# Quarter-array products in the inverse of a delta-rule layer, and another order of work in its steps

## The reference, cut to what matters

```
def step(s, inp):
    r_t, w_t, k_t, v_t, kk_t, a_t = inp
    sa = jnp.einsum('bhvk,bhk->bhv', s, -kk_t)
    s = s * w_t[:, :, None, :] + sa[..., None] * (kk_t * a_t)[:, :, None, :] + v_t[..., None] * k_t[:, :, None, :]
    return s, jnp.einsum('bhvk,bhk->bhv', s, r_t)

o_f, s_f, k_f = direction(0, False, s_f0)
o_b, s_b, k_b = direction(1, True, s_b0)
o = o_f + o_b
```

## Time and profile before

| | us |
|---|---|
| median of 3 runs (1657.66 to 1657.81) | 1657.73 |
| the profiled execution | 1657.09 |
| its span, first to last instruction | 1655.3 |
| TensorE busy / VectorE / ScalarE / GpSimd in the span | 1465.5 / 605.6 / 528.1 / 264.7 |
| mean granted TensorE clock | 0.948 |
| the block of this change | 881 to 1235 |
| one pair of heads in the middle of it | 42.9 |

### The profile page before, as it was taken

How to read it: one execution, slowest core, us unless ns; L and a number is a source line. 1 busy time by engine, 2 the same in 40 slices (tenths; PEclk the granted TensorE clock), 3 DMA queues, 4 the chain that set the end, 5 groups by cost and what they waited for, 6 DMA issues and landing times. The chain is left out here.

```text
span 1655.3 us, 41184 instructions
## 1 busy us (share of the span) xinstructions
PE 1465.5 (89%) x17678; PEld 930.4 (56%) x17678; DVE 605.6 (37%) x1520; ACT 528.1 (32%) x1202; POOL 264.7 (16%) x260
## 2 busy tenths in 40 slices
PE   3998878878999999959998888888879779999997
PEld 1554557446555555535556777777755555555554
DVE  2003673243111111551214666666751511111116
ACT  3013553232121121220134666666541311111122
POOL 0000031002000000010034455556500100000010
PEclk9999899888999999979999999999988889999999
DMA  9324556737799999803210000000004469999992
GB/s 390 128 102 164 221 210 244 300 115 315 278 369 379 374 377 373 332 26 102 103 50 3 6 6 6 6 6 6 6 4 170 154 267 364 374 370 380 375 387 90
DMA packets 54037, 328.34 MB, mean 198 GB/s; under 512 B 6646, under 2 KB 10038, under 8 KB 18712
## 3 DMA queue, kind: packets, MB, share of 16 engines
q1 hardware_dynamic: 43632, 290.07, 45.9%
q0 software_dynamic: 5184, 18.88, 2.9%
q10 hardware_dynamic: 5096, 17.58, 2.7%
HBM read 304.35 MB, written 22.16 MB: 197 GB/s over the span
## 5 line engine op out<-in xcount | busy, mean ns | idle before, releaser
L1398 PE MATMUL ps<-ring,arena 128*64 128x256 f32 x2048 | 244.3, 387 | 6.0 <-ACT arena L1513 4.9
L1398 PEld LDWEIGHTS ps<-ring,arena 128*64 128x64 f32 x2048 | 142.4, 138 | 97.2 <-issue 36.6
L298 PE MATMUL ps<-HT,ring 128*128 128x384 f32 x544 | 181.3, 497 | 14.2 <-PEq L367 8.2
L298 PEld LDWEIGHTS ps<-HT,ring 128*128 128x128 f32 x544 | 105.8, 195 | 89.5 <-issue 20.3
L1408 PE MATMUL ps<-ring,arena 128*32 128x128 f32 x4096 | 133.9, 278 | 0.0
L1602 DVE TENSOR_TENSOR arena<-arena,ps 64x256 f32<-64x256 f32 (+1 forms) x128 | 40.6, 357 | 254.0 <-ACT arena L1519 254.0
L1434 PE MATMUL ps<-ring,arena 128*64 128x512 f32 x512 | 129.9, 605 | 0.0
L1518 ACT ACTIVATE arena<-ps 64x256 f32<-64x256 f32 x64 | 24.1, 377 | 311.3 <-PE ps L1398 311.3
L1408 PEld LDWEIGHTS ps<-ring,arena 128*32 128x32 f32 x4096 | 107.8, 111 | 27.0 <-issue 25.4
L298 PE MATMUL ps<-arena,ring 128*128 128x384 f32 x256 | 85.4, 498 | 18.8 <-DVEq L2053 18.8
L1526 ACT ACTIVATE arena<-ps 32x256 f32<-32x256 f32 x128 | 47.8, 374 | 160.3 <-PE ps L1434 159.2
(11 more groups left out here) (358 smaller groups left out, 2244.2 us busy)
## 6 DMA issues: line engine op xcount, KB each, us to landing
ring<-wstream SPq DMA_DIRECT2D x272, 1024.0 KB, 7.5
moe_rows<-arena ACTq DMA_DIRECT2D x28, 384.0 KB, 7.1
arena<-moe_tokens POOLq DMA_DIRECT2D x12, 512.0 KB, 14.7
moe_rows<-arena ACTq DMA_DIRECT2D x4, 512.0 KB
consts<-cst ACTq DMA_DIRECT2D x1, 1655.0 KB, 17.1
XT<-xT ACTq DMA_DIRECT2D x1, 1536.0 KB, 11.1
yT<-HT SPq DMA_DIRECT2D x3, 384.0 KB, 3.2
arena<-wa SPq DMA_DIRECT2D x1, 1024.0 KB, 4.9
```

Of the source, the lines that this page charges most:

```text
L298: mm = pe.matmul(bank(m % 8), w[:, k, m % 2 * P:m % 2 * P + P], rhs[:, k, :], start=k == 0, stop=k == KC - 1)
L1398: mm = pe.matmul(bank(h, 256)[HD * x:HD * x + HD], TOKE[:, k, 0:MANY], w[:, kk, x, :], start=k == 0, stop=k == KC - 1)
```

## The change

Five edits, all in this block.

1. `each` on halves of the array (12 matmuls, 64 rows, 64 columns out) becomes `quarters_pe`: 24 matmuls, each 32 rows by 32 columns, on the four tiles of the array's diagonal in turn; quarter q takes block q % 2 of head q // 2.
2. The masks of levels 1 to 4 are compacted once at the block's start from two 32-column halves to one (`LM`, 8 additions on VectorE), and `left_dve` and `right_dve` read and write 32 columns a chunk where they had 64.
3. ScalarE's decays of step 0 stand ahead of the copies L2226 and L2230 and not behind them.
4. In the steps of VectorE, the block masks of the next pair (L2318), the first sums (L2330, L2331), the addition of the unit matrix (L2335) and the transposition (L2336) stand in other places.
5. `first_level_dve` is cut in two, so that the transposition (`first_turn_dve`) has its own place.

```diff
+        PF = area(take(T), T, d=2, n=NCH, j=32)
+        LM = area(take(8 * 32), 8 * 32, v=4, d=2, j=32)
...
 def inverse_act
                     last.then_inc(s_vr, 1)
+                act.wait_ge(s_si[c % 2], c // 2 * 32 + 32)
+                act.wait_ge(s_zc, c + 1)
+                decays_act(act, c, 0)
                 act.wait_ge(s_inv, c * NINV + NINV - 2)
...
 def left_dve
-                mask = msk1(C_LEV + 2 * (n - 1) * CH, d)
-                dve.tensor_tensor(dn(PF)[:, d].rearrange("p n (b j) -> p n b j", b=2),
-                                  bank(LEFT_BANKS[d], NCH * HD).rearrange("p (n b j) -> p n b j", b=2, j=32),
-                                  mask.rearrange("p n (b j) -> p n b j", b=2), ALU.mult).then_inc(s_ls, 1)
+                dve.tensor_tensor(PF[:, d], p_, LM[:, n - 1, d].unsqueeze(1).broadcast_to([P, NCH, 32]),
+                                  ALU.mult).then_inc(s_ls, 1)
...
 def steps_dve, with s the step
                     if nx is not None:
                         if s == 2:
-                            blocks_dve(dve, nx, 1)
+                            first_sums_dve(dve, nx, 0)
                         if s == 3:
+                            first_turn_dve(dve, 0)
                             first_sums_dve(dve, nx, 1)
                     dve.wait_ge(s_so, c * 4 + (s + 1))
...
                     if nx is not None:
+                        if s == 1:
+                            blocks_dve(dve, nx, 0)
                         if s == 2:
-                            first_sums_dve(dve, nx, 0)
+                            first_level_dve(dve, 0)
                         if s == 3:
                             first_level_dve(dve, 1)
+                            first_turn_dve(dve, 1)
...
-                    if nx is not None:
-                        if s == 1:
-                            blocks_dve(dve, nx, 0)
-                        if s == 2:
-                            first_level_dve(dve, 0)
+                    if nx is not None and s == 1:
+                        blocks_dve(dve, nx, 1)
...
-            def each(pe, o, left, right, d):
+            def quarters_pe(pe, o, left, right, d):
                 for n in range(NCH):
-                    for h in halves:
-                        mm = pe.matmul(bank(o, HD, HD * n)[h].rearrange("p (b j) -> p b j", b=2), dn(left)[h, d, n],
-                                   right[h, d, n].unsqueeze(1).broadcast_to([HD, 2, 32]), start=True, stop=True)
+                    for q in range(4):
+                        rows = slice(32 * q, 32 * q + 32)
+                        mm = pe.matmul(bank(o, 32, 32 * n)[rows], left(rows, n, q % 2), right[rows, d, n], start=True, stop=True)
                 return mm
```

More of the change, by code:

```diff
@@ L1812, in build @@
         assert a_[0] == KC * T
-        ATF, PF, ODF = (area(take(U2), U2) for _ in range(3))
+        ATF = area(take(U2), U2)
+        PF = area(take(T), T, d=2, n=NCH, j=32)
+        LM = area(take(8 * 32), 8 * 32, v=4, d=2, j=32)
+        take(T - 8 * 32)
+        ODF = area(take(U2), U2)
         AB, BK = (area(take(2 * U2), 2 * U2, g=2, d=2, n=NCH, i=CH) for _ in range(2))
@@ L2231, in inverse_act, with decays_act @@
                                    bank(x, 4 * P).rearrange("p (m g k) -> p g m k", g=2, k=HD), ACT.Copy).then_inc(s_bk, 1)
+            def decays_act(act, c, s):
+                for g in range(2):
+                    for a, d, n in lanes_at(s):
+                        last = act.activation(next_state(s, g, a), ZV[halves[g], g, FIRST[s] + a], ACT.Copy,
+                                              scale=EW[halves[g], c % 2, d, n:n + 1])
+                last.then_inc(s_zd, 1)
             def steps_act(act, c, nx, j):
@@ L2237, in steps_act @@
                     w, x = len(ln), FIRST[s]
-                    if s:
+                    if s in (1, 2):
                         act.wait_ge(s_zu, c * 3 + s)
[L2240 to L2250, removed]
+                        if s == 1 and c:
+                            act.wait_ge(s_po[(c - 1) % 2], (c + 1) // 2 * 16)
+                        decays_act(act, c, s)
                     act.wait_ge(s_so, c * 4 + (s + 1))
@@ L2361, in right_dve @@
                 dtc, dc = (v[:, d].rearrange("p n j -> p (n j)") for v in (DTC, DC))
-                once = bank(RIGHT_BANKS[d], NCH * HD).rearrange("p (n b j) -> p n b j", b=2, j=32)[:, :, 0]
-                dve_o(dve.tensor_tensor(DTC[:, d], DTC[:, d], once, ALU.subtract))
+                dve_o(dve.tensor_tensor(dtc, dtc, bank(RIGHT_BANKS[d], NCH * 32), ALU.subtract))
                 dve.transpose(dc, dtc).then_inc(s_inv, 1)
@@ L2434, in _ @@
                 dve_o.inc(dve.memset(DTF, 0.0))
+                dve.wait_ge(s_xm, 6)
+                for n in range(1, NLEV):
+                    for d in range(2):
+                        at = C_LEV + 2 * (n - 1) * CH + d * CH
+                        dve_o.inc(dve.tensor_tensor(LM[:, n - 1, d], C[:, at:at + 32], C[:, at + 32:at + CH], ALU.add))
                 for d in range(2):
@@ L2439, in _ @@
                     first_level_dve(dve, d)
+                    first_turn_dve(dve, d)
                 for c in range(KC):
@@ L2491, in left_pe @@
                 if n < NLEV:
-                    mm = each(pe, LEFT_BANKS[d], AF, DC, d)
+                    mm = quarters_pe(pe, LEFT_BANKS[d], lambda rows, m, i: dn(AF)[rows, d, m, 32 * i:32 * i + 32], DC, d)
                 else:
@@ L2504, in right_pe @@
                 if n < NLEV:
-                    mm = each(pe, RIGHT_BANKS[d], PF, DTC, d)
+                    mm = quarters_pe(pe, RIGHT_BANKS[d], lambda rows, m, i: PF[rows, d, m], DTC, d)
                 else:
@@ L2509, in right_pe @@
                             k, i = HD * g + 32 * d, HD * g + 32 * (1 - d)
-                            mm = pe.matmul(bank(RIGHT_BANKS[d], 32, 32 * m)[k:k + 32], dn(PF)[i:i + 32, d, m, 0:32],
+                            mm = pe.matmul(bank(RIGHT_BANKS[d], 32, 32 * m)[k:k + 32], PF[i:i + 32, d, m],
                                            DTC[i:i + 32, d, m], start=True, stop=True)
```

5 lines of the change are left out of this document (3 added, 2 removed).

## The result

| us | before | after |
|---|---|---|
| median | 1657.77 (4 runs) | 1678.68 (4 runs, 1675.44 to 1687.3) |
| ratio, 95% interval | | 1.0132 (1.0094 to 1.017) |
| the profiled execution / its span | 1657.09 / 1655.3 | 1678.41 / 1676.6 |
| mean granted TensorE clock | 0.948 | 0.927 |
| instructions | 41184 | 47328 |

A forecast was written before the change was run, and what follows sets the result against it. The prediction took a chain passing from engine to engine as the bound. Six middle pairs gaining 2.7 us, the first 2.1 and the last 1.4 made 6.2 us off 1657.09, so 1651 us, range 1643 to 1660.

The forecast's parts named there:

- the sum: Whole block: a middle pair gains 0.45 us, six of them 2.7, first pair 2.1, last 1.4; together 6.2 us.
- (7): Sign to look for in the profile: a middle pair takes 42.4 to 42.5 us.
- the stretch from level 5 to the steps: Level 5's first product to the steps' first: bounded by ScalarE's gapless list, expected to stay the same.
- Rival C: No change: gain and loss equal, or TensorE's clock falls, costing perhaps 3 to 5 us; 1656 us, chance 0.19.
- One product, 0.50 us: Each level product: 48 records on four tiles take 0.50 us, 0.34 us less than on halves.
- The masks, 0.34 us: VectorE's compacted level masks take about 0.34 us, 0.2 us less each; the eight additions for `LM` cost nothing.
- Level 2, 3.92 us: First crossed product to lora products: two tile shapes no longer overlap, 3.92 us, a loss of 0.67 us a pair.
- Level 4, 1.0 us gained: Level 4's first product to level 5's: shorter products and masks let level 5 start 1.0 us earlier.
- Decays of step 0, zero: ScalarE's list before the half solution: moving the decays ahead gains zero, between -0.1 and +0.2 us.
- Steps, +0.1: Steps and level 1: first sums wait for GpSimd, level 1 wins it back, 0.1 us gained; unstalled, 0.8 us.
- (5): Sign to look for: the first sum in step 2 takes 0.9 to 1.3 us beside GpSimd's L1977.
- Rival B: Every level product: four diagonal quarters run no faster than two; 1.3 us lost per pair, 1668 us, chance 0.14.

The follow-up runs named there:

- e5: The changed kernel with each quarter product moving 64 columns instead of 32, same records, tiles and order; 1666.3 us, ratio 1.0047 to before.
- e11: e5 with the first right product of the first pair done ten times in a row; ran once, bursts of 128 records each 3.46 us, no kernel time given.
- e10: e2 with the products of levels 3 and 4 on quarters moving 64 columns; 1651.05 us, ratio 0.9978 to before.
- e9: e2 with only level 4's products on quarters moving 64 columns; 1648.24 us, ratio 0.9947 to before.
- e3: The kernel before, its half products moving 32 columns once instead of twice, VectorE's mask reading them twice; 1711.53 us, ratio 1.0316.
- e13: e2 with only level 4's products on quarters moving 32 columns; 1657.25 us, ratio 0.9992 to before.
- e8: The kernel before with ScalarE's new order alone, the decays of step 0 ahead of the block's copies; 1652.18 us, ratio 0.9968.
- e7: The kernel before with VectorE's new order in the steps alone (masks, first sums, first turn); 1650.09 us, ratio 0.9953.
- e2: The kernel before with the new order of ScalarE and VectorE alone, products left on halves; 1646.72 us, ratio 0.9926.
- e14: e2 with the products of levels 1 and 4 on quarters moving 32 columns; 1653.52 us, ratio 0.9978 to before.
- e12: e2 with the first right product of the first pair, on halves, done ten times in a row; ran once, 264 records in 8.2 us, no kernel time given.
- e4: The kernel before with 11 matmuls of one column added to each level product on halves; 1778.09 us, ratio 1.0715.

## Why the prediction was wrong

The forecast of 1651 us was wrong in sign, and the step that failed is the sum: "A middle pair: 0.1 + 1.0 - 0.67 = 0.45 us gained" (the terms themselves make 0.43). It held for a clock of 1.00 and for instructions that are always there. A pair took 44.1 to 47.9 us and not the 42.5 of (7); 46.5 on average; seven times 4.0 is 28 us, the whole difference between forecast and result. Two terms carry it: the 1.0 us gained in level 4, where 0.6 was lost, and a term that the prediction left at nothing, the stretch from level 5 to the steps, for which it looked at ScalarE's list alone. It was to stay at 4.95 us and took 8.06, since TensorE ran most of it at 1.2 GHz.

- **The clock.** Rival C named it, with 3 to 5 us for "a tenth more of the block at that level". In the seven pairs the mean clock fell from 0.97 to 0.86, which is nearly a quarter more of the time at 1.2 GHz. The stretch from level 5 to the steps alone gives 3.1 us a pair, 22 us over seven: as much as the kernel lost against before. That is the greater part. e5 beside the changed kernel gives 12 us, with three pairs still under 1.00; but its longer products also ask for fewer instructions a microsecond, so that this is not the clock's share alone. Nothing in the earlier trace rows showed that it would fall. The pairs of before with clock 0.96 took 1.0 us more than those at 1.00:

```profile
1024.13:1067.11 42.98, 37.36 (x849) 30.22 (x848) 30.42 (x76) 28.65 (x64) 25.32 (x22) 1.00 0.02 5
1067.11:1110.99 43.88, 38.56 (x849) 31.52 (x848) 30.54 (x75) 29.56 (x65) 25.33 (x22) 0.96 0.02 6
```

  From this slope alone 0.86 would have meant 3.5 us a pair, an estimate.
- **Supply.** No part of the prediction asked whether 6144 more instructions arrive in time. It took the rate from the earlier trace rows, 24 records that had waited for VectorE and lay ready, and carried it over to sixteen products of 48 a pair. By e11 the supply is 74 instructions a microsecond; the product asks for 96 in 0.54 us. Its direct price at full clock is 0 to 0.9 us a pair, from e10 beside e9. It may cost more through the clock: the two pairs of e5 at 0.93 have a level 4 of 5.53 and 5.75 us, but its first pair, with 5.57, is at 1.00. How much of the low clock in the changed kernel comes from these waits and how much from the narrow products, no run separates; e3 and e13 show that the narrow products are enough.
- **One product, 0.50 us.** 0.54 to the next, wider product at 2.4 GHz. Right. The rule of the Trainium skill (TensorE: Matmul & The Clock Gate, Back-to-back issue gap) with its floor of about 25 ns is not borne out across tiles: 11 ns a record here (45 for each of the four tiles), 15.5 in e11. Four row tiles wrote one PSUM bank at that rate, nearly twice that of two tiles in the earlier trace rows, so that the rule of the Trainium skill (TensorEngine Tiling (Array Packing), Gotcha 1: PSUM Pressure) does not show here either.
- **The masks, 0.34 us.** 0.32 to 0.36. Right. That the eight additions for `LM` cost nothing was wrong: they take 2.34 us, and the first block mask stands 2.9 us behind the clearing of the ring instead of 2.3, 0.6 us once.
- **Level 2, 3.92 us.** 4.01 in six pairs. Right: the two tile shapes don't overlap here.
- **Level 4, 1.0 us gained.** 0.8 at full clock (e13). In the changed kernel it lost 0.6 on average, since its records waited on issue and ran at 1.2 GHz in part.
- **Decays of step 0, zero.** 0.24 us a pair (e8). The list is as full as the prediction said, but both halves of the solution waited until the decays had ended (1047.46; ScalarE's half started at 1047.55, VectorE's L2410 at 1047.57). In e8 copies stand there, ScalarE's half starts 0.13 us ahead of the end of the last one, and VectorE's 0.58 us ahead of ScalarE's.
- **Steps, +0.1.** At full clock VectorE's order gains 0.6 (e7), beside the 0.8 that the prediction gave for a sum that is not stalled, and both orders 0.8 (e2). With level 4 shortened the sum is stalled, and of 0.8 from the orders and 0.8 from level 4 only 0.8 is left (e13). In the changed kernel level 4 gained nothing, and the sum took 0.32 to 0.36 in all 16 cases. So (5) did not come true, though e13 shows its mechanism.
- **Rival B** gave the nearest time, 1668, by luck, for a reason that is not so: with its instructions there, a product of 48 records took 0.54 us and not 0.9.

At full clock and with few added instructions the sum nearly stands: with levels 1 and 4 narrow and the new orders a pair takes 41.80 us (e14), 1.18 less than before. Less 0.76 for level 2 that makes 0.42 us a pair, an estimate from e14, the kernel before and the changed one; by the prediction 0.45. The prediction's terms were right for a clock that didn't stay.

## What to carry to other kernels

Before a product is cut into more and smaller matmuls, count the instructions, weight loads included, over the stretch in which they must arrive, and compare with the rate at which the instruction queue has delivered; idle time on "issue" inside a burst is the sign in a profile, and packets of the instruction queue at their shortest distance are another. Work on the array that looks wasted may be what keeps TensorE at 2.4 GHz: where a change takes columns away in a chain with many waits, look at the granted clock by stage first, also in the stretches behind the change, and keep the columns if they cost next to nothing, as here (0.03 us a product). And a gain ahead of a point where two engines meet is worth no more than the slack of the other one; put the shorter products behind it.

## What the runs showed that was not expected

- Moving half the columns made the kernel 53 us slower with the same instructions (e3), at a granted clock of 0.73 to 0.77 in every pair.
- As much as the changed kernel lost stands behind its changed products: 8.06 us instead of 4.95 from level 5 to the steps, most of it at 1.2 GHz.
- On two 64 by 64 tiles in turn a record takes 30 to 32 ns whether it moves 64, 32 or 1 column (e12, e3, e4).
- A packet of 16 KB holds 256 of TensorE's instructions and arrived each 3.46 us in the steady state (e11).
- A VectorE operation with both inputs in SBUF, beside a GpSimd operation of the same kind, ends 0.21 us behind it (e13: 1.21 us instead of 0.35), as L2335 did in the earlier trace rows.
